# Entering a token-major product while the column form still runs, exponentials written out, four banks for the first table pass

## The reference, cut to what matters

```python
def sq_relu_mlp(h, w_in, w_out):                       # w_in 1024 x 4096, w_out 4096 x 1024
    return jnp.square(jax.nn.relu(h @ w_in)) @ w_out

def chunk_fn(xc):                                      # in peer(); 128 tokens at a time
    ...                                                # top 16 of 16 x 16 key pairs, per head
    w = jax.nn.softmax(cv, axis=-1)
    u = u_tab[eidx]
    a = jax.nn.gelu(jnp.einsum('td,thkd->thk', xc, u, preferred_element_type=f32)) * w
    return jnp.einsum('thk,thkd->td', a.astype(v_tab.dtype), v_tab[eidx])
```

## Time and profile before

| | us |
|---|---|
| median of 3 runs | 2953.02 (2951.01 to 2953.20) |
| the profiled execution | 2951.89 |
| its span | 2950.2 |
| PE busy | 2817.8 (96%) |
| weight loads (PEld) busy | 2517.7 (85%) |
| DVE busy | 1989.1 (67%) |
| ACT busy | 1482.9 (50%) |
| mean granted TensorE clock | 0.982 of full |

### The profile page before, as it was taken

How to read it: one execution, slowest core, us unless ns; L and a number is a source line. 1 busy time by engine, 2 the same in 40 slices (tenths; PEclk the granted TensorE clock), 3 DMA queues, 4 the chain that set the end, 5 groups by cost and what they waited for, 6 DMA issues and landing times.

```text
span 2950.2 us, 51661 instructions
## 1 busy us (share of the span) xinstructions
PE 2817.8 (96%) x17556; PEld 2517.7 (85%) x17556; DVE 1989.1 (67%) x3725; ACT 1482.9 (50%) x2397; POOL 489.1 (17%) x390
## 2 busy tenths in 40 slices
PE   8889998999999989999999999999899999999998
PEld 6679887788789889999988888785899999988886
DVE  4557975679965759866866666516479848766666
ACT  2444454544443444667855555205245668745554
POOL 0000100011100000477700000000000787400000
PEclk9999999999999999999999999989999999999999
DMA  8638973489854445666556666540355775566663
GB/s 283 209 116 260 346 252 112 128 243 355 331 171 129 143 143 177 176 174 157 137 178 215 214 215 213 126 143 15 93 176 178 178 174 135 145 212 216 215 213 131
DMA packets 355204, 547.85 MB, mean 186 GB/s; under 512 B 71073, under 2 KB 251681, under 8 KB 354466
## 3 DMA queue, kind: packets, MB, share of 16 engines
q1 hardware_dynamic: 303618, 471.46, 50.3%
q0 software_dynamic: 51488, 75.11, 9.8%
HBM read 545.33 MB, written 15.84 MB: 190 GB/s over the span
## 4 chain that ended last, share of the span: by engine, by line
PE 90%; DVE 4%; ACT 3%; DMA 2%; issue 1%; ACTq 0%; SPq 0%; DVEq 0%
PE ps L1002 34%; PE ps L929 12%; PE ps L933 12%; PE ps L930 12%; PE ps L980 4%; PE ps L1369 2%; DMA tile_ring<-mlp_w_in 1%; PE ps L1490 1%; PE ps L904 1%; PE ps L1132 1%; PE ps L863 1%; PE ps L1579 1%; PE ps L874 1%; PE ps L964 1%; PE ps L1030 1%
## 5 line engine op out<-in xcount | busy, mean ns | idle before, releaser
L929 PE MATMUL ps<-x_high,w_high 128*128 128x256 f32 x3264 | 819.2, 288 | 28.5 <-DVE x_low L2730 10.6
L930 PE MATMUL ps<-x_low,w_high 128*128 128x256 f32 x3264 | 805.1, 284 | 0.0
L929 PEld LDWEIGHTS ps<-x_high,w_high 128*128 128x128 f32 x3264 | 628.5, 193 | 41.3 <-issue 26.0
L800 POOL DMA_INDIRECT by_key<-spare x256 | 420.1, 1641 | 1330.3 <-DVE spare L2805 1216.0
L930 PEld LDWEIGHTS ps<-x_low,w_high 128*128 128x128 f32 x3264 | 629.8, 193 | 0.4
L2231 DVE TENSOR_TENSOR w_low<-tile_ring,w_high 128x1024 fp32r<-128x1024 f32 x256 | 313.8, 1226 | 249.4 <-ACT w_high L1821 249.4
L933 PE MATMUL ps<-x_high,w_low 128*128 128x256 f32 x3264 | 460.8, 284 | 1.4 <-DVE w_low L3026 1.4
L1821 ACT ACTIVATE w_high<-tile_ring 128x1024 fp32r<-128x1024 f32 x256 | 271.5, 1061 | 346.0 <-PE ps L1002 346.0
L933 PEld LDWEIGHTS ps<-x_high,w_low 128*128 128x128 f32 x3264 | 423.9, 193 | 1.6 <-DVE w_low L3026 1.6
L1002 PE MATMUL ps<-w_high,x_high 128*128 128x512 f32 x1440 | 389.9, 393 | 21.2 <-DVE x_low L2186 16.7
L1964 ACT ACTIVATE w_high<-tile_ring 128x1024 fp32r<-128x1024 f32 x256 | 270.7, 1058 | 262.9 <-PE ps L933 215.5
(11 more groups left out here) (365 smaller groups left out, 3253.2 us busy)
## 6 DMA issues: line engine op xcount, KB each, us to landing
tile_ring<-peer_u SPq DMA_DIRECT2D x256, 512.0 KB
tile_ring<-peer_v SPq DMA_DIRECT2D x256, 512.0 KB
arena<-mod_w POOLq DMA_DIRECT2D x112, 512.0 KB, 6.4
tile_ring<-mlp_w_in SPq DMA_DIRECT2D x64, 512.0 KB
tile_ring<-mlp_w_out SPq DMA_DIRECT2D x64, 512.0 KB
tile_ring<-ret_w_in SPq DMA_DIRECT2D x48, 512.0 KB
tile_ring<-peer_w_q SPq DMA_DIRECT2D x32, 512.0 KB
by_key<-zero_rows POOLq DMA_DIRECT2D x16, 896.0 KB, 5.1
```

The costliest lines, as they stand in the source:

```text
L800: pool.indirect_dma_start(out=flat, out_offset=bass.IndirectOffsetOnAxis(ap=slot_at[0:SCATTER, n:n + 1], axis=0), in_=slot_weight[0:SCATTE ...
L929: nc.tensor.matmul(dst, cols, x_high[:, c, :], start=c == 0, stop=False)
L930: nc.tensor.matmul(dst, cols, x_low[:, c, :], start=False, stop=False)
```

## The change

A small tile `first_chunk` is added: two parts of 128 x 256, laid over the start of `route`. There are three edits.

First, the token-major product is entered earlier. Before the last unit's square (MLP) or the last gelu (table pass) ACT rounds the first weight tile into `w_high` and the first chunk into `first_chunk`. DVE makes the two low parts before the last unit's relu (MLP), or between the merges of tile 125 and tile 126 (table pass). PE's first twelve matmuls read `first_chunk`, and its wait for all units is replaced by a wait at each of the four banks' first matmuls.

Second, the sums of the first table pass go to banks 4, 5, 6 and 7 in turn, and PE waits for the gelu four tiles back instead of two.

Third, the exponentials stand inside a written-out group of four tiles, behind the rounding copy of tile 34 (and 66) and ahead of the gelu of tile 32 (and 64).

```diff
-RAISED_AT = (36, 68)
+RAISED_AT = (32, 64)
...
+            first_chunk = first_chunk_life.enter_context(nc.sbuf_tensor("first_chunk", [P, 2, T], F32R))
...
+                        xh, xl = x_high[:, k, :], x_low[:, k, :]
+                        if begun and opening and k == 0:
+                            xh, xl = first_chunk[:, 0, :], first_chunk[:, 1, :]
...
+                                    if begun and opening and k == 0 and i == 0:
+                                        pe.wait_ge(*begun(2 * b + half))
...
-                pe.wait_ge(hidden_ready, hidden.up(FF // 2))
-                split_token_rows(FF)
+                hidden.up(FF // 2)
+                split_token_rows(FF, lambda bank: (hidden_ready, hidden.n - FF // 2 + 1))
...
-                    a = k % 2
-                    if begun or k >= 2:
-                        pe.wait_ge(gate_stored, j * RING + (t0 + k - 1))
+                    if begun:
+                        pe.wait_ge(gate_stored, j * RING + (t0 + k - RING + 1))
...
-                    column_products(ps[:, 4 + a, 0:T], a, (high_ready, at), (low_ready, at)).then_inc(act_sums, 1)
+                    column_products(ps[:, 4 + k % RING, 0:T], k % 2, (high_ready, at), (low_ready, at)).then_inc(act_sums, 1)
...
-                split_token_rows(P)
+                split_token_rows(P, lambda bank: (gate_stored, t0 + P - RING + 1 + bank))
...
+                def closing():
+                    act.wait_ge(tile_loaded[0], 16 * (n0 // RING + 1))
+                    A(w_high[:, 0, :], tile_ring[:, 0, :], ACT.Copy).then_inc(high_ready, 1)
+                    act.wait_ge(hidden_ready, r0 + 1)
+                    A(first_chunk[:, 0, :], h1[:, 0, :], ACT.Copy).then_inc(row_high, 1)
...
+                        if closing and not ahead and q == BANKS - 1:
+                            act.wait_ge(tile_used, p0 + count)
+                            closing()
                         if tail:
                             tail(q, j, begun)
...
-                def tiles(j):
+                def tiles(j, raise_block=None):
                     for k in range(RING):
                         high(k + 2, j)
+                        if k == 0 and raise_block:
+                            raise_block()
                         gelu(k, j)
...
-                    act.wait_ge(routed, TB * l + b + 1)
-                    A(route[:, b, 2, :], route[:, b, 2, :], ACT.Exp).then_inc(pick_exp, 1)
-                    j0 = RAISED_AT[b] // RING
+                    def raise_block():
+                        act.wait_ge(routed, TB * l + b + 1)
+                        A(route[:, b, 2, :], route[:, b, 2, :], ACT.Exp).then_inc(pick_exp, 1)
+                    tiles(RAISED_AT[b] // RING, raise_block)
+                    j0 = RAISED_AT[b] // RING + 1
...
+                act.wait_ge(tile_loaded[0], 16 * (split.n // RING + 1))
+                A(w_high[:, 0, :], tile_ring[:, 0, :], ACT.Copy).then_inc(high_ready, 1)
+                act.wait_ge(gate_weighed, l * P + 1)
+                A(first_chunk[:, 0, :], gates[:, 0, :], ACT.Copy).then_inc(row_high, 1)
+                gelu_apart(P - 1, 0)
...
+            def enter_rows(src, at):
+
+                v.wait_ge(high_ready, at + 1)
+                V.tensor_tensor(w_low[:, 0, :], tile_ring[:, 0, :], w_high[:, 0, :].bitcast(F32), ALU.subtract).then_inc(low_ready, 1)
+                v.wait_ge(row_high, row_highs.n + 1)
+                V.tensor_tensor(first_chunk[:, 1, :], src[:, 0, :], first_chunk[:, 0, :].bitcast(F32),
+                                ALU.subtract).then_inc(x_cut, 1)
...
-                for k in (3, 2, 1):
-                    merge(P - k)
-                chunk(0, 0)
+                merge(P - 3)
+                enter_rows(gates, n0)
+                merge(P - 2)
+                merge(P - 1)
...
+                body(0, entered=True)
```

More of the change, by code:

```diff
@@ L1771, in high_columns, with token_rows @@
                 pairs.up(count)
-            def token_rows(src, count, rows0, cleared, each=None, between=None):
+            def token_rows(src, count, rows0, cleared, each=None, between=None, entered=False):
                 n0, r0 = split.n, row_highs.n
@@ L1817, in body @@
                     for k in range(2 * RING):
[L1818 to L1823 removed]
+                        if begun or k >= 1:
+                            act.wait_ge(tile_loaded[k % RING], j * 32 + 16 * (n0 // RING + k // RING + 1))
+                            if begun or k >= 2:
+                                act.wait_ge(panel_used, j * (2 * RING) + (rows0 + k - 1))
+                            A(w_high[:, k % 2, :], tile_ring[:, k % RING, :], ACT.Copy).then_inc(high_ready, 1)
                         if k + 1 < 2 * RING or ahead:
@@ L2025, in peer @@
                 weigh_tiles(n_it - 1, ahead=False)
-                for k in range(RING):
+                for k in range(RING - 1):
                     if k + 2 < RING:
@@ L2140, in copy_tokens, with low_columns @@
                 return lambda i, u: V.tensor_copy(dst[:, :, bass.ds(i * 256, 256)], bank2(u))
-            def low_columns(count, op, done=unit_done, taken=unit_taken, looped=True, beside=None, opened=None, first=None):
+            def low_columns(count, op, done=unit_done, taken=unit_taken, looped=True, beside=None, opened=None, first=None, closing=None):
                 n0, u0 = split.n, units.n
@@ L2199, in body @@
                             behind_row(j * RING + k)
-                chunk(0, 0)
+                if entered:
+                    body(0, entered=True)
+                else:
+                    chunk(0, 0)
                 if behind_row:
@@ L2204, in token_rows @@
                 elif count > RING:
-                    with v.Fori(0, count // RING - 1) as j:
+                    with v.Fori(1 if entered else 0, count // RING - 1) as j:
                         body(j)
@@ L2238, in weighed_rows @@
                     weigh(k, 0)
-                for k in (3, 2, 1):
-                    merge(P - k)
-                chunk(0, 0)
+                merge(P - 3)
+                enter_rows(gates, n0)
+                merge(P - 2)
+                merge(P - 1)
                 n_it = P // (2 * RING)
-                with v.Fori(0, n_it - 1) as j:
+                body(0, entered=True)
+                with v.Fori(1, n_it - 1) as j:
                     body(j)
@@ L2603, in cross_and_mlp @@
                     v.wait_ge(c_ready, 1)
-                low_columns(FF // 2, relu_of, beside=modulation(1 + l), opened=opened, first=scale_ready)
+                n1 = split.n + FF
+                low_columns(FF // 2, relu_of, beside=modulation(1 + l), opened=opened, first=scale_ready,
+                            closing=lambda: enter_rows(h1, n1))
                 made.up((FF // 2) * (1 + l))
-                token_rows(h1, FF, beside=modulation(1))
+                token_rows(h1, FF, beside=modulation(1), entered=True)
                 made.up(FF)
```

55 lines of the change are left out of this document (28 added, 27 removed).

## The result

| us | before | after |
|---|---|---|
| median | 2952.02 (2949.69 to 2953.20, 4 runs) | 2926.22 (2920.75 to 2931.04, 4 runs) |
| profiled execution | 2951.89 | 2925.27 |
| its span | 2950.2 | 2923.6 |

The ratio is 0.9914, with a 95% interval of 0.9898 to 0.9930: faster by 0.9%. The forecast was 2926.0 in 2921 to 2937. A second set of four runs of the same kernel gave 2923.63 (0.9906, interval 0.9890 to 0.9921).

The account below looks back on a forecast made before the run. PE bounds 90% of the chain, so only its standing or lower-clock time can be won. 13.2 + 4.2 + 2.1 + 7.3 = 26.8 us off the profiled 2951.89 gives 2925.1, median 2926; eight-in-ten range 2921 to 2937.

Parts of the forecast that it names:

- First table pass, 13.2 us: Both layers' first table pass: four banks and written-out exponentials remove PE's stalls, 13.2 us, bounds 10 to 13.6.
- The working of 5.4 against 5.76 us: At an exponential: ACT's copy, loads, exponential, gelu and next copy take 5.4 us; PE needs that copy at 5.76.
- The drain of the Trainium skill's page: Page's rule: each table switch costs about 1.38 us beyond the load; exponentials would stall PE some 2.4 us, sum 3.6.
- Rival 3: First table pass wins little, the exponentials stalling PE as before; 13.6 us remain, 2939; chance 0.07.
- First MLP, 4.2 us: Entry of its second product: 2.6 us from an earlier start, 1.6 from the clock staying up; bounds 1 and 4.9.
- Second table pass, 2 x 3.65 us: Entry in each layer: 1.95 us from an earlier start, 1.7 from the clock; sum 7.3, bounds 2 x 1 and 2 x 4.
- Second MLP, 2.1 us: Entry of its second product: PE starts 2.1 us earlier, gap still 2.3, nothing counted for the clock; bounds 0 and 3.5.
- What the clock is worth at the second MLP: At its entry: nothing counted, since with the clock up DVE would hold the second tile.
- Rival 1: At the entries the clock falls all the same; 5.0 us are not won, 2931; chance 0.09.
- Rivals 2 and 5: 2: entries win nothing, DVE late for second tile, 2940, 0.09 including partly. 5: bank cycling lowers first pass's clock, 3052, 0.01.
- Rival 4: MLPs' second products: DMA takes over, rate at or below 337 GB/s, slower at 2959; chance 0.04.
- Its signs of being wrong: A gap at an entry's second tile, clock 0.50 behind a gap below 1 us, or a tile's DMA wait in the MLPs.

Follow-up runs that it names:

- banks_only: Kernel before with only the first table pass's four banks and the wait for the gelu four tiles back: 2938.38 us, ratio 0.9950.
- entry_only: Kernel before with only the four early entries, two banks and the old exponentials: 2937.51 us, ratio 0.9955.
- the filler: Kernel before with nine unread matmuls in PE's gap ahead of each second table pass: 2946.76 us, ratio 0.9987.
- late_mods: Changed kernel with the last unit's two modulations of the second MLP put behind its second product: 2926.43 us, ratio 0.9907.
- the repeat: The changed kernel run once more, nothing altered: 2923.63 us, ratio 0.9906.
- The filler's 6.52: Changed kernel with nine unread matmuls in PE's gap at the entry of the second MLP's second product: 2922.56 us, ratio 0.9906.
- early_pair: Changed kernel with ACT's and DVE's entry work at both MLPs moved one unit earlier, before unit 14's modulations: 2928.10 us, ratio 0.9914.
- late_again: Second run of the changed kernel with the second MLP's last two modulations behind its second product: 2926.39 us, ratio 0.9914.
- exp_only: Kernel before with only the exponentials written out inside the tile groups, two banks: 2948.99 us, ratio 0.9993.
- early_late: Changed kernel with MLP entry work one unit earlier and the second MLP's last two modulations behind its second product: 2924.52 us, ratio 0.9909.

## Why the prediction was right, step by step

- **What bounds the kernel: right.** All that was won is time in which PE stood or ran at the lower level of its clock.
- **First table pass, 13.2 us: right, 13.6** (6.74 and 6.82 by the stretches of banks_only, 6.83 and 6.80 from tile 0 to 87). The tiles took 251.21 us, with 251.4 forecast, and the residual stall of 0.1 us per exponential is zero. The attribution was too generous to the third edit. The prediction gave the exponentials' 6.8 us to the written-out order together with the banks; with the banks alone they go too, and with the written-out order alone these waits grow, and only 3.7 us are won in both passes. The working of 5.4 against 5.76 us is correct, but it describes a case that four banks would have forgiven anyway.
- **The drain of the Trainium skill's page (ScalarE: Activation LUTs, What ACT_TABLE_LOAD costs): not seen.** The exponential starts 1.29 us behind the start of its load here as before, and the gelu 1.30 behind its own (1192.12 and 1193.42). Rival 3, which the drain would have made true, stays out. The prediction's sum for that case is a little off: stalls of 2.4 us instead of 0.1 at four exponentials leave 4.0 us of the 13.2, not 3.6.
- **First MLP, 4.2 us: right, 4.7 by the stretch.** The gap is 0.57 us where 0.65 was forecast, and the first tile takes 2.87 us.
- **Second table pass, 2 x 3.65 us: right in both halves.** 1.95 us were forecast for the earlier start; entry_only shows 1.95 and 2.11. 1.7 were forecast for the clock; the passes show 1.58 and 1.55, and the filler shows what they hang on. That the clock had fallen in both passes of before is itself a matter of chance in part: behind the same gap it fell in seven of eight.
- **Second MLP, 2.1 us: the gap right, the gain not.** The gap went from 4.40 us to 2.30 and 2.04, with 2.2 to 2.5 forecast. But the stretch lost only 0.8 and 1.0 us. Of the rest, 0.5 and 0.8 us are a longer column stage. Nothing is edited up to the last unit. The profiles with the old entry differ by 1.2 us there, and entry_only and late_mods, with the new one, lie among them, so it is most likely chance. The other 0.8 and 0.3 us are the step that was mis-sized, "so 2.1 is nearly all there is". It put the second tile at nothing behind a low clock. In the first profile PE waited there for the low part, which stood on DVE behind a modulation that had waited 1.14 us for its tile. In the repeat two modulations waited 0.33 and 0.60, and the third tile's low part was late. The waits for modulated tiles are what the prediction left out.
- **What the clock is worth at the second MLP: next to nothing, as the prediction had it, or up to 1.2 us.** With the clock up the third tile starts 7.30 us behind the entry in entry_only, and DVE holds PE at the second tile for 0.35 and 0.81 us. With the clock low it is 7.73 and 7.18 in the changed kernel. The filler's 6.52 is counted from an entry that it had itself put off.
- **Rival 1 (the clock falls all the same): wrong** at the short gaps, right at the one of 2.3 us, as the prediction's own step had it.
- **Rivals 2 and 5: wrong.** No second tile stalled at the first MLP or the table passes; rival 2 held in part in the one place above. With four banks in turn the tiles kept 2.88 us, so no sign of the clock going up and down was seen. early_pair shows that rival 2 does become true one unit earlier.
- **Rival 4: wrong in the MLPs' second products**, which take from the third tile on what they took before: 87.0 us in the first MLP and 94.5 in the second. Transfers do set the pace in the column stage ahead of it, where the prediction had not looked.
- **Its signs of being wrong.** Two of them did show: a wait at the second tile of the second MLP's entry (0.25 us), and waits for transfers in the MLPs (the modulation's 1.14 us, and 14.5 us of ACT's copies for `w_in` tiles). The second sign was ill chosen, since ACT had 15.2 us of these waits before.
- **The sum.** 26.8 us were forecast; the profiles have 26.6, the medians 25.8, and in the second set 27.6. The closeness is partly luck: the second MLP gave 1.3 us less, the untouched places gave 2.9 - 3.4 = -0.5 and 0.9 in small pieces. The other terms came out at 25.5, with 24.7 forecast.

What stays open: why the transfer of the last `w_in` tile is late in some profiles and not in others. One kernel showed both (late_mods and late_again).

## What to carry to other kernels

Before an activation's place or its table loads are rearranged, try a deeper ring of PSUM banks behind it: here two more banks hid all 54 loads and won 13.6 us, the rearrangement alone won 3.7 us by its trace, and on top of the banks it won nothing. At a switch from one product to the next prepare the first operands ahead of the last piece of the old product, and price the gap and the tile behind it separately, since the gap of 2.27 us cost another 1.6 us in the clock in seven entries of eight. One step earlier is not better: in an engine that works in order it only moves the wait to the second tile. Where transfers set the pace just ahead of the entry, as in the second MLP's column stage, its length and the gap behind it differ by 1 to 2 us from profile to profile. One profile can't price a change of that size; cut the stretch into pieces and compare each over several profiles.

## What the runs showed of the hardware

- The clock at the start of a token-major product went with the length of PE's gap, but not by length alone. In all fourteen profiles together it stayed up in each of 86 starts behind 0.18 to 1.78 us (twelve matmuls in 2.80 to 2.88 us where nothing else waited). Behind 2.04 to 2.30 us it fell in ten of eleven (4.30 to 4.42 us), behind 2.81 us in four of fourteen, and behind 3.25 to 4.40 us in all ten (4.12 to 5.26 us).
- In code of another shape it fell behind 1.73 us (exp_only), and within an entry behind 1.87 us (early_late). One group of 16 matmuls stands behind a gap of 1.98 us four times in each profile; it took 5.41 us in 19 of the 56 cases and 3.72 in the others.
- Matmuls whose result nobody reads kept the clock up: the next tile took 2.84 instead of 4.41 us.
- The same 96 matmuls ahead of the first MLP took 22.02 to 22.07 us in ten profiles, and 24.93, 23.59, 23.48 and 23.40 in four, in code that no edit touches. All stand behind a gap of 2.81 us, and in the four the clock fell there (0.50 in the window of before). Three of the four are the profiles of the kernels with the late modulations, so it may be more than chance; no run tells. A difference of 3 us between two profiles can be that alone.
- ACT took a table load, an exponential, a second load and a gelu in a row at 1.29, 0.33 and 1.30 us from start to start, with no further pause.
